# A third probability buffer, two rounds of lead and a fused masked maximum in the second block's attention

## Chip, cores and metric

The kernel is one program on one core of a Trainium2 chip, in fp32 throughout. The metric is the device time of one execution in microseconds, as the median of three runs.

## The reference, cut to what matters

The reference runs a first block (pooled mixing with chunk attention, a Mamba2 mixer, two mixture-of-experts layers) and then a second block of two layers. The change touches only the windowed attention of the second block's layers, and in layer 0 the attention of the 256 context positions, which the kernel treats as two more query tiles.

```python
def windowed_gqa(q, k, v, k_ctx, v_ctx, sink):        # 8 query heads, 2 key heads, head width 64
    # 4 query blocks of 128; keys: the block before, this one, the one after
    s_loc = jnp.einsum('bnqhgd,bnkhd->bnhgqk', qb, kw) * scale            # scale = 64 ** -0.5 = 0.125
    s_loc = jnp.where(mask, s_loc, NEG_INF)                # |key - query| <= 128, inside the sequence
    s_ctx = jnp.einsum('bnqhgd,bchd->bnhgqc', qb, k_ctx) * scale          # 256 context keys
    p = jax.nn.softmax(jnp.concatenate([s_loc, s_ctx, s_sink], axis=-1), axis=-1)
    o = einsum(p_loc, vw) + einsum(p_ctx, v_ctx)           # the sink has a share of p and no value
def context_attention(q, k, v, sink):                  # layer 0 only: 256 queries, 256 context keys
    p = jax.nn.softmax(jnp.concatenate([q k * scale, s_sink], axis=-1), axis=-1)[..., :L]
```

The same layers hold a depthwise convolution of 31 taps, gates (`att_z` among them, a product of the layer's input with a weight), retention, a short convolution and a merged output.

## The kernel before

Every engine runs its own program, written out by hand in program order; engines wait for each other by counting semaphores. A helper (`job`) hands out the eight PSUM banks of 512 columns in rotation: a new job waits until the bank's previous holder has been read.

The attention runs in rounds (n, j): a tile n of 128 queries and a key head j, which serves four query heads. Layer 0 has 12 rounds (4 sequence tiles, 2 context tiles, times 2 key heads), layer 1 has 8. Tiles 1 and 2 see three local key tiles, tiles 0 and 3 two, context tiles none; all see two context key tiles. PE's program per round (from L1310 on): scores of the next round (`att_scores`, L1294: a local part `sl`, L1304, and a context part `sx`, L1308, each a bank for each of the four heads), one part of the gate product `att_z` (L1290), then for each head the transposes of its normalised probabilities (L1330, two banks for each head), then the product with V (L1338, 64 output columns, into partitions 0 to 63 of one bank for each round).

DVE's program per round: `att_norm` (add the sink's exponential to the sums, L2128, reciprocal, L2930, scale each head's probabilities, L2124), `att_max` of the next round (for each head scale and add the mask, L2131, scale the context part, L2124; then one reduction over all four heads, L2134, the maximum with the sink, and two small results), three or four taps of the convolution of channel group 3 (`conv`, L2131), and now and then a gate product (L2131). ACT's program per round (L1980 on): the gate product's tanh and copy (`z_part_out`), copies of the transposes from PSUM to SBUF (L1575, two for each head), the four exponentials of the next round with their sums (L1567, each followed by a read of the accumulator), and two copies of the round's V product (L1575). All work in place in `pr2[r % 2]`, a buffer of 4 x 640 columns.

After the last round DVE makes the weight sums (`w_sums`, `w_sum_4`) and activation sums T1 to T4 of the next stage, whose first products (L716) PE starts at once.

Of the kernel before, what the change touches and what calls it, by code (L numbers as in the profile page):

```python
# [188 lines left out]
def program(nc, a, out, upto, old, new):  # L189

    ctx = ExitStack()
    with ctx:
# [18 lines left out]
        square = sb("square", [P, 2, S + L])  # L211
        rstd = sb("rstd", [P, S + L])
        part_sum = sb("part_sum", [P, 2, 3 * P])
# [257 lines left out]
        kd = mQ.take(2, S + L)  # L471
        k_raw = mQ.take(S + L)
        v_tok = mQ.take(6, P)
        cu = mQ.take(2, 813)
        pT2 = mQ.take(5, S)
        v_raw = arena[:, mQ.at - 5 * S:mQ.at - 5 * S + S + L]
        pr2 = [mQ.take(4, 640), None]
# [122 lines left out]
        def x_tiles(l):  # L600
            return range(6 if l == 0 else 4)

        def tile_at(n):

            return P * n
# [44 lines left out]
        def _(eng):  # L650
# [580 lines left out]
            if stage_on(6):  # L1231
                eng.wait_ge(small_landed, pe.at("small"))
                for l in range(2 if upto > 6 else 1):
# [59 lines left out]
                    def att_scores(n, j, z=()):  # L1293
                        for hh in range(4):  # L1294
                            if hh == 1:
                                for c, tag in z:
                                    z_bank[c, tag] = z_job(c, tag)
                            h = 4 * j + hh
                            po, c = 64 * (h % 2), h // 2
                            ql = q_[po:po + 64, c, n * P:(n + 1) * P]  # L1300
                            kt = key_tiles(n)
                            if kt:
                                b, full = job("sl", l, h, n)
                                nc.tensor.matmul(b[:, 0:P * len(kt)], ql,  # L1304
                                                        kd[po:po + 64, j, P * kt[0]:P * (kt[-1] + 1)],
                                                        start=True, stop=True).then_inc(tensor_done, pe.step(full))
                            b, full = job("sx", l, h, n)
                            nc.tensor.matmul(b[:, 0:L], ql, kd[po:po + 64, j, S:S + L], start=True, stop=True).then_inc(tensor_done, pe.step(full))  # L1308

                    z_bank = {}  # L1310
                    att_scores(*rounds[0])
                    for c, tag in z_parts(l, 0):
                        z_product(c, tag, *z_job(c, tag))
                    for r, (n, j) in enumerate(rounds):
                        if r + 1 < len(rounds):
                            att_scores(*rounds[r + 1], z=z_parts(l, r) if r else ())
                            for c, tag in z_parts(l, r) if r else ():
                                z_product(c, tag, *z_bank[c, tag])
                        kt = key_tiles(n)
                        nl = len(kt)  # L1320
                        for hh in range(4):
                            h = 4 * j + hh
                            eng.wait_ge(vector_done, pe.at(("pr2", l, n, h)))
                            pr = pr2[r % 2][:, hh, :]
                            for tag, t0, t1 in (("l", 0, nl), ("x", nl, nl + 2)):
                                if t1 == t0:
                                    continue
                                b, full = job("pt2", l, h, n, tag)
                                for t in range(t0, t1):
                                    mm = nc.tensor.transpose(b[:, (t - t0) * P:(t - t0 + 1) * P], pr[:, t * P:(t + 1) * P],  # L1330
                                                             C("ident"))
                                mm.then_inc(tensor_done, pe.step(full))
# [2041 lines left out]
```

## Time and profile before

| | us |
|---|---|
| median of 3 runs | 3477.21 (3474.63 to 3478.76) |
| span of the profiled execution, its own time in the profile | 3482.4 |
| PE busy | 3282.0 (94%) |
| DVE busy | 1790.9 (51%) |
| ACT busy | 901.8 (26%) |
| GpSimd busy | 287.3 (8%) |

PE is TensorE's matmul row, PEld its weight loads, DVE VectorE, ACT ScalarE. An fp32 matmul is two records in the trace, a transpose one. A record's time is longer than its slot, since matmuls are pipelined; the start of one to the start of the next is the slot. The profiled execution has no time beside its span; it lies 5.2 us above the median of the runs.

### The profile page before, as it was taken

The numbers are of one execution on the slowest core, as the hardware profiler recorded it, in microseconds if no ns is written. First come the engines' busy times: TensorE is split into PE (matmuls) and PEld (weight loads), VectorE is DVE, ScalarE is ACT, GpSimd is POOL, SyncE is SP. The second block draws the span as 40 slices with busy tenths as digits, with TensorE's granted clock in tenths as the row PEclk, the third lists the DMA queues.
The fourth block names the chain that finished last, engine by engine and source line by source line (L and its number), as shares of the span: only waits on it lengthen the run. The fifth ranks groups of instructions, "written<-read, shape, count | busy, mean of one in ns | idle before, by whom it ended". The sixth has DMA issues, their size and how long they took to land.

```text
span 3482.4 us, 36840 instructions
## 1 busy us (share of the span) xinstructions
PE 3282.0 (94%) x13516; PEld 2085.1 (60%) x13516; DVE 1790.9 (51%) x3363; ACT 901.8 (26%) x1855; POOL 287.3 (8%) x246
## 2 busy tenths in 40 slices
PE   8988989999998989989999999999999899999998
PEld 4743544778744545555555555555544556778887
DVE  2343226777713337777334454444468854554554
ACT  2241212344312221054231131111112523222222
POOL 1200421333101320000000000000000000000000
PEclk9988999999998999999999999999999999999999
DMA  8746876533355972101111212112221021222331
GB/s 271 227 138 204 341 272 214 176 86 97 115 174 202 363 269 61 37 13 41 37 49 39 58 43 66 56 55 61 61 64 58 19 65 45 65 72 80 85 91 61
DMA packets 418494, 394.00 MB, mean 113 GB/s; under 512 B 27888, under 2 KB 353648, under 8 KB 410896
## 3 DMA queue, kind: packets, MB, share of 16 engines
q1 hardware_dynamic: 384768, 348.01, 31.6%
q10 hardware_dynamic: 15120, 23.68, 2.1%
q0 software_dynamic: 18432, 19.98, 1.7%
q8 instruction: 111, 1.82, 0.2%
q14 instruction: 63, 0.52, 0.0%
HBM read 440.78 MB, written 31.52 MB: 136 GB/s over the span
## 4 chain that ended last, share of the span: by engine, by line
PE 61%; DVE 5%; ACT 3%; DMA 2%; issue 1%; ACTq 0%; DVEq 0%; POOL 0%; POOLq 0%
PE psum L716 38%; PE psum L701 6%; PE psum L1204 3%; PE psum L914 2%; DVE arena L2131 2%; PE psum L1290 2%; PE psum L1338 2%; ACT arena L1575 2%; DMA ring<-in_w_branch 1%; PE psum L933 1%; PE psum L1358 1%; PE psum L1370 1%; DVE arena L2128 1%; ACT arena L1567 1%; PE psum L899 1%
## 5 line engine op out<-in xcount | busy, mean ns | idle before, releaser
L716 PE MATMUL psum<-arena,ring 128*128 128x384 f32 (+1 forms) x2592 | 747.2, 439 | 12.8 <-DVE arena L2128 5.3
L716 PEld LDWEIGHTS psum<-arena,ring 128*128 128x128 f32 x2592 | 492.3, 191 | 238.6 <-DVE psum L2128 11.4
L716 PE MATMUL psum<-hT,ring 128*128 128x384 f32 (+1 forms) x2176 | 624.9, 440 | 2.3 <-ACT part_sum L1575 2.2
L716 PEld LDWEIGHTS psum<-hT,ring 128*128 128x128 f32 x2176 | 414.8, 191 | 192.7 <-issue 7.8
L1575 ACT ACTIVATE part_sum<-psum 128x256 f32<-128x256 f32 (+1 forms) x408 | 174.2, 429 | 953.4 <-PE psum L716 808.5
L2128 DVE TENSOR_TENSOR ring<-ring 128x512 f32<-128x512 f32 (+1 forms) x336 | 215.9, 662 | 260.1 <-PE psum L716 257.4
L2128 DVE TENSOR_TENSOR psum<-psum,part_sum 128x256 f32<-128x256 f32 (+1 forms) x328 | 156.2, 479 | 371.5 <-PE psum L716 262.7
L1575 ACT ACTIVATE arena<-psum 128x256 f32<-128x256 f32 (+5 forms) x501 | 210.5, 465 | 506.7 <-PE psum L701 188.8
L701 PE MATMUL psum<-hT,ring 128*128 128x512 f32 (+1 forms) x832 | 314.7, 540 | 14.1 <-DVE hT L2124 11.8
L1567 ACT ACTIVATE arena<-psum,cols 128x256 f32<-128x256 f32 (+3 forms) x280 | 131.7, 493 | 636.0 <-PE psum L914 195.3
L701 PEld LDWEIGHTS psum<-hT,ring 128*128 128x128 f32 x832 | 160.9, 194 | 167.8 <-issue 149.2
L2131 DVE SCALAR_TENSOR_TENSOR arena<-arena,vec 128x783 f32<-128x783 f32 (+1 forms) x256 | 228.7, 894 | 9.1
L2128 DVE TENSOR_TENSOR arena<-arena 128x512 f32<-128x512 f32 (+13 forms) x252 | 187.4, 757 | 58.1 <-DMA arena<-y_dram 18.4
L2131 DVE SCALAR_TENSOR_TENSOR arena<-arena,psum 128x384 f32<-128x384 f32 (+3 forms) x236 | 98.5, 447 | 217.2 <-ACT arena L1567 183.0
L1567 ACT ACTIVATE arena<-arena,cols 128x512 f32<-128x512 f32 (+8 forms) x199 | 158.6, 830 | 59.5 <-DVE arena L2131 24.5
L989 PE MATMUL psum<-hT,ring 128*128 128x256 f32 x672 | 154.4, 381 | 0.0
L989 PEld LDWEIGHTS psum<-hT,ring 128*128 128x128 f32 x672 | 126.4, 190 | 19.8 <-issue 3.4
L2128 DVE TENSOR_TENSOR arena<-psum,part_sum 128x384 f32<-128x384 f32 (+1 forms) x80 | 40.8, 510 | 164.1 <-PE psum L716 163.8
L716 PE MATMUL psum<-arena,square 128*128 128x384 f32 (+1 forms) x384 | 115.4, 436 | 3.8 <-DVE arena L2128 3.8
L1204 PE MATMUL psum<-arena,ring 128*128 128x512 f32 x256 | 111.8, 595 | 0.0
L914 PE MATMUL psum<-arena 128*64 128x256 f32 x960 | 108.8, 380 | 1.0 <-issue 1.0
L2131 DVE SCALAR_TENSOR_TENSOR xT<-psum,cols,xT 128x512 f32<-128x512 f32 (+1 forms) x64 | 37.7, 612 | 137.4 <-PE psum L1204 73.3
(255 smaller groups left out, 3693.3 us busy)
## 6 DMA issues: line engine op xcount, KB each, us to landing
ring<-in_w_in SPq DMA_DIRECT2D x172, 512.0 KB, 4.1
arena<-in_moe_w SPq DMA_DIRECT2D x44, 1536.0 KB
ring<-in_ada_w SPq DMA_DIRECT2D x96, 512.0 KB, 6.1
ring<-in_w_mod SPq DMA_DIRECT2D x48, 512.0 KB, 5.8
ring<-in_ssm_w_in SPq DMA_DIRECT2D x48, 512.0 KB, 5.5
ring<-in_w_branch SPq DMA_DIRECT2D x64, 256.0 KB, 3.1
hT<-in_moe_w SPq DMA_DIRECT2D x10, 1536.0 KB
ring<-in_moe_w SPq DMA_DIRECT2D x10, 1024.0 KB
```

What stands on the lines that cost most here:

```text
L701: mm = nc.tensor.matmul(b[:, 0:n], ws[k // 8][0][:, k % 8, :], rhs(k)[:, o:o + n], start=(k == 0), stop=(k == nk - 1))
L716: mm = nc.tensor.matmul(flat(bank_, nb), lhs[:, k, :], rhs(k), start=(start and k == 0), stop=(k == kd_ - 1), skip_group_check=True)
L899: mm = nc.tensor.transpose(b[:, j * P:(j + 1) * P], rows[:, i % DEEP, k * P:(k + 1) * P], C("ident"))
L914: mm = nc.tensor.matmul(b[LANES * h:LANES * h + LANES, 0:2 * P], rowsT[:, i % 2, k, LANES * h:LANES * h + LANES], step_weights(s, h, 2 * P ...
L989: mm = nc.tensor.matmul(bank_[:, 0:S // 2], lhs[:, k, :], rhs(k), start=(start and k == 0), stop=(k == 3), skip_group_check=True)
L1204: mm = nc.tensor.matmul(b, ws[k // 8][0][:, k % 8, :], yT[:, k, :], start=(k == 0), stop=(k == 15))
L1290: mm = nc.tensor.matmul(b[:, 0:w], z_w[c][0][:, k, :], hT[:, k, o:o + w], start=(k == 0), stop=(k == KD - 1))
L1338: mm = nc.tensor.matmul(b[0:64, :], v_tok[:, t, 64 * j:64 * j + 64], pT2[:, kb, :], start=(i == 0), stop=(i == len(tiles) - 1))
L1567: return nc.scalar.activation(out_, in_, f, bias=bias, scale=scale, **kw)
L1575: return nc.scalar.activation(out_, in_, ACT.Copy)
L2128: return v.tensor_tensor(out_, in0, in1, op)
L2131: return v.scalar_tensor_tensor(out_, in0, s, in1, op0, op1)
```

## The change

PE keeps two rounds of scores ahead instead of one; `pr2` gets a third buffer, over scratch that other stages use (`square`, `rstd`, part of `part_sum`, now one allocation). The context scores of four heads share two banks. Transposes go to one bank for each key tile, with the four heads side by side, so a bank is full only when the last head is done. ACT copies one bank of 512 columns for each key tile. The V product is made once for each tile, for both key heads, into the two halves of the partitions. On DVE one instruction scales, adds the mask, writes the scores and gives their running maximum, which starts from the sink (local part) or from the local part's maximum (context part, with a mask of zeros). The convolution taps and the gate product stand before `att_max`. ACT's `z_part_out` stands behind the exponentials. After the last round, T1 and T2 stand before the weight sums. The diff's core:

```diff
+        pT_window = arena[:, k_raw_at:k_raw_at + 3 * S].rearrange("p (a b) -> p a b", b=S)
+        pT_context = w_sum.rearrange("p m n -> p (m n)")[:, 0:2 * S].rearrange("p (a b) -> p a b", b=S)
+        pr2 = [mQ.take(4, 640), None, scratch[:, 0:4 * 640].rearrange("p (a b) -> p a b", b=640)]
...
+        def pr_no(l, r):
+            return (r + l) % 3
+        def pT2(j, kb):
+            return pT_first[:, kb, :] if j == 0 else pT_window[:, kb, :] if kb < 3 else pT_context[:, kb - 3, :]
...
+                    def att_turns(r, n, j):
+                        tiles = att_tiles(n)
+                        banks = [job("pt2", l, n, j, kb) for kb, t in tiles]
+                        for hh in range(4):
+                            eng.wait_ge(vector_done, pe.at(("pr2", l, n, 4 * j + hh)))
+                            for i, (b, full) in enumerate(banks):
+                                mm = nc.tensor.transpose(b[:, hh * P:(hh + 1) * P], pr2[pr_no(l, r)][:, hh, i * P:(i + 1) * P], C("ident"))
+                                if hh == 3:
+                                    mm.then_inc(tensor_done, pe.step(full))
+                    def att_values(n):
+                        tiles = att_tiles(n)
+                        b, full = job("av", l, n)
+                        for i, (kb, t) in enumerate(tiles):
+                            for j in range(2):
+                                eng.wait_ge(scalar_done, pe.at(("ptc2", l, n, j, kb)))
+                                mm = nc.tensor.matmul(b[64 * j:64 * j + 64, :], v_tok[:, t, 64 * j:64 * j + 64], pT2(j, kb),
+                                                      start=(i == 0), stop=(i == len(tiles) - 1), skip_group_check=True)
+                    att_scores(*rounds[1])
                     for r, (n, j) in enumerate(rounds):
+                        att_turns(r, n, j)
+                        if r + 2 < len(rounds):
+                            att_scores(*rounds[r + 2])
+                        for c, tag in z_parts(l, r) if r else ():
+                            z_product(c, tag, *z_job(c, tag))
+                        if j:
+                            att_values(n)
...
+                        for kb, t in att_tiles(n):
+                            jn = jobname("pt2", l, n, j, kb)
+                            eng.wait_ge(tensor_done, ac.at(("full",) + jn))
+                            copy(pT2(j, kb), bank(jn)).then_inc(scalar_done, ac.step([("free",) + jn, ("ptc2", l, n, j, kb)]))
                         if r + 1 < len(rounds):
                             att_exp(r + 1, *rounds[r + 1])
+                        if r:
+                            z_part_out(z_parts(l, r))
...
-                                stt(pr2[q][:, hh, 0:wl], b[:, 0:wl], 0.125, C("window", off, wl), ALU.mult, ALU.add).then_inc(vector_done, ve.step(free))
...
-                            ts(pr2[q][:, hh, wl:wl + L], b[:, 0:L], 0.125).then_inc(vector_done, ve.step(free))
...
-                        red(col("stat", 32 * q, 4), pr2[q][:, :, 0:wl + L], ALU.max).then_inc(vector_done, ve.step())
...
-                        tt(col("stat", 32 * q, 4), col("stat", 32 * q, 4), sink, ALU.max).then_inc(vector_done, ve.step())
+                            v.tensor_tensor_reduce(pr[:, hh, 0:wl], b[:, 0:wl], C("window", off, wl), 0.125, col("small", 16 + 8 * l + 4 * j + hh),
+                                                   ALU.add, ALU.max, top(hh)).then_inc(vector_done, ve.step([free, ("top", l, n, j, hh)]))
...
                         att_norm(r, n, j)
-                        if r + 1 < len(rounds):
-                            att_max(r + 1, *rounds[r + 1])
                         conv(3, taps * r, taps * r + taps)
...
+                        if r + 2 < len(rounds):
+                            att_max(r + 2, *rounds[r + 2])
```

## Rows read from the trace of the kernel before

**Rows 1.** The page's busy time of each engine over the span.
```profile
PE 3282.0 (94%) x13516; PEld 2085.1 (60%) x13516; DVE 1790.9 (51%) x3363; ACT 901.8 (26%) x1855; POOL 287.3 (8%) x246
```

**Rows 2.** Busy time by stretch: attention of layer 0, of layer 1.
```profile
core 0: us, PE busy (x) PEld busy (x) DVE busy (x) ACT busy (x) POOL busy (x), PEclk, DMA share, GB/s
1473.70:1625.50 151.80, 132.81 (x616) 85.23 (x616) 120.18 (x240) 76.34 (x234) 0.00 (x0) 0.98 0.05 15
2675.00:2791.30 116.30, 102.58 (x468) 64.85 (x465) 92.69 (x184) 57.43 (x166) 0.00 (x0) 0.96 0.06 19
```

**Rows 3.** Waits from 1503 to 1625 us: who for whom, total us, times, longest.
```profile
ACT arena L1567 <- PE psum L1290: 50.3, 10, 8.0
DVE cols L2128 <- ACT cols L1567: 21.1, 10, 3.6
PE psum L1338 <- ACT arena L1575: 12.1, 11, 1.3
PE psum L1330 <- ACT arena L1575: 3.3, 6, 0.6
```

**Rows 4.** Timeline of PE over a round: start, us, engine, line, operation, records.
```profile
1519.10 2.08 PE L1330 MATMUL psum<-const,arena 128*128 128x128 f32 x17 [0.51 <-ACT arena L1575]
1522.24 4.48 PE L1338 MATMUL psum<-arena 128*64 128x512 f32 x10 [1.07 <-ACT arena L1575]
1526.65 0.92 PE L1304 MATMUL psum<-arena 64*128 64x384 f32 x4
...
1529.11 3.72 PE L1290 MATMUL psum<-hT,ring 128*128 128x256 f32 x16
...
1533.67 0.55 PE L1330 MATMUL psum<-const,arena 128*128 128x128 f32 x3 [0.51 <-ACT arena L1575]
```

**Rows 5.** Timeline of PE: two-half products of an expert stage, one-half product of tile 3.
```profile
1170.79 1.94 PE L933 MATMUL psum<-arena 128*64 128x512 f32 x8
1172.56 3.62 PE L914 MATMUL psum<-ring,arena 128*64 128x256 f32 x32
...
1591.00 3.62 PE L1338 MATMUL psum<-arena 128*64 128x512 f32 x8 [1.25 <-ACT arena L1575]
```

**Rows 6.** Timeline of DVE over a round.
```profile
1511.04 0.16 DVE L2128 TENSOR_TENSOR cols<-cols 128x4 f32<-128x4 f32 x1 [3.63 <-ACT cols L1567]
...
1513.30 0.55 DVE L2131 SCALAR_TENSOR_TENSOR arena<-psum,const 128x384 f32<-128x384 f32 x1
1513.77 0.41 DVE L2124 TENSOR_SCALAR arena<-psum 128x256 f32<-128x256 f32 x1
...
1516.61 2.82 DVE L2134 TENSOR_REDUCE cols<-arena 128x4 f32<-128x2560 f32 x1
1519.46 0.16 DVE L2128 TENSOR_TENSOR cols<-cols 128x4 f32<-128x4 f32 x1
...
1519.92 3.17 DVE L2131 SCALAR_TENSOR_TENSOR arena<-arena,vec 128x783 f32<-128x783 f32 x3
1523.01 0.95 DVE L2131 SCALAR_TENSOR_TENSOR arena<-arena 128x768 f32<-128x768 f32 x1
```

**Rows 7.** Groups of DVE by line and form in a routing stage (mean ns last).
```profile
L2465 DVE TENSOR_TENSOR_SCAN arena<-arena,psum 32x512 f32<-32x512 f32 x1 | 1.2, 1207 | 0.7 <-PE psum L861 0.7
...
L2131 DVE SCALAR_TENSOR_TENSOR arena<-arena 32x512 f32<-32x512 f32 x1 | 0.7, 737 | 0.0
```

**Rows 8.** Timeline of ACT: a copy of 512 columns, one exponential, its read, the next.
```profile
1422.36 0.60 ACT L1575 ACTIVATE arena<-psum 128x512 f32<-128x512 f32 x1 [20.95 <-PE psum L701]
...
1521.82 0.87 ACT L1567 ACTIVATE arena<-arena,cols 128x640 f32<-128x640 f32 x1
1522.54 0.24 ACT L1567 ACTIVATION_READ_ACCUMULATOR arena<-arena,cols 128x1 f32 x1
1522.63 0.86 ACT L1567 ACTIVATE arena<-arena,cols 128x640 f32<-128x640 f32 x1
```

**Rows 9.** Timeline of PE: first transposes and next stage's first product, both layers.
```profile
1487.47 2.67 PE L1330 MATMUL psum<-const,arena 128*128 128x128 f32 x16 [0.89 <-DVE arena L2131]
...
1625.55 5.43 PE L716 MATMUL psum<-hT,ring 128*128 128x384 f32 x16
...
2688.77 2.66 PE L1330 MATMUL psum<-const,arena 128*128 128x128 f32 x16 [0.89 <-DVE arena L2131]
...
2791.31 3.72 PE L716 MATMUL psum<-hT,ring 128*128 128x256 f32 x16
```

More of the change, by code:

```diff
@@ new lines, in att_turns @@
+                    def att_turns(r, n, j):
[6 more added lines that the diff above has]
+                                if hh == 3:
+                                    mm.then_inc(tensor_done, pe.step(full))
@@ new lines, in att_values @@
+                    def att_values(n):
[6 more added lines that the diff above has]
+                                                      start=(i == 0), stop=(i == len(tiles) - 1), skip_group_check=True)
+                        mm.then_inc(tensor_done, pe.step(full))
@@ L1998, in _ @@
                         if r + 1 < len(rounds):
                             att_exp(r + 1, *rounds[r + 1])
-                        jn = jobname("av", l, n, j)
-                        eng.wait_ge(tensor_done, ac.at(("full",) + jn))
-                        bv = bank(jn)[0:64, :].rearrange("p (a b n) -> p a b n", a=2, b=2)
-                        for half in range(2):
-                            copy(br[64 * half:64 * half + 64, 12 + 2 * j:14 + 2 * j, tile_at(n):tile_at(n) + P],
-                                 bv[:, :, half, :]).then_inc(scalar_done, ac.step([("free",) + jn, ("att_o", l)]))
+                        if r:
+                            z_part_out(z_parts(l, r))
@@ new lines, in _ @@
+                        if j:
+                            jn = jobname("av", l, n)
+                            eng.wait_ge(tensor_done, ac.at(("full",) + jn))
+                            for jj in range(2):
+                                bv = bank(jn)[64 * jj:64 * jj + 64, :].rearrange("p (a b n) -> p a b n", a=2, b=2)
+                                for half in range(2):
+                                    copy(br[64 * half:64 * half + 64, 12 + 2 * jj:14 + 2 * jj, tile_at(n):tile_at(n) + P],
+                                         bv[:, :, half, :]).then_inc(scalar_done, ac.step([("free",) + jn, ("att_o", l)]))
@@ L2922, in att_max @@
-                        tt(col("stat", 32 * q + 12, 4), sink, col("stat", 32 * q, 4), ALU.subtract).then_inc(vector_done, ve.step(("nm2", l, n, j)))
+                        if r >= 3:
+                            eng.wait_ge(tensor_done, ve.at(("full",) + jobname("pt2", l, *rounds[r - 3], 4)))
+                        top = lambda hh: col("stat", 16 * q + hh)
+                        sink = col("small", 16 + 8 * l + 4 * j, 4)
+                        for hh in range(4 if kt else 0):
+                            off = P * (kt[0] - (n - 1))
+                            b, free = full("sl", l, 4 * j + hh, n)
+                            v.tensor_tensor_reduce(pr[:, hh, 0:wl], b[:, 0:wl], C("window", off, wl), 0.125, col("small", 16 + 8 * l + 4 * j + hh),
+                                                   ALU.add, ALU.max, top(hh)).then_inc(vector_done, ve.step([free, ("top", l, n, j, hh)]))
```

137 lines of the change are left out of this document (49 added, 88 removed).

## The prediction

> **What bounds the kernel now.** I read the page first: TensorE (PE) is busy for 94% of the span, VectorE (DVE) 51%, ScalarE (ACT) 26% [rows 1]. Those are averages. The change touches only the second block's attention, twice: 151.8 us in its layer 0 and 116.3 us in its layer 1. The table by stretches shows DVE at 120.2 and 92.7 us busy there, so two engines are loaded and not one [rows 2]. The waits of layer 0 give the pattern of a round (one tile of 128 queries, one key head): ACT waits for a gate product on PE, DVE waits for the exponentials, PE waits for the copies that ACT makes of the transposes [rows 3]. PE's own order shows the price: a full round repeats every 14.57 us (1519.10 to 1533.67), of which PE loses 0.51 and 1.07 us; the rest is transposes, 4.48 us for the product with V, 2.46 us of scores (1526.65 to 1529.11) and 3.7 us of gate product [rows 4]. So a shorter DVE or a longer lead alone can return about 1.6 us of a round; more must come from less PE work.
>
> **Less PE work: the product with V.** Its matmuls have 64 output columns. Now both key heads write partitions 0 to 63, one round after the other, and ten records of 512 columns take 4.48 us, 0.448 each [rows 4]. After, the two heads write the two halves of one bank, in turns, every second round. The trace has that form elsewhere: eight records of 512 columns into alternating halves take 1.94 us against 3.62 us for eight of one half, and 32 of 256 take 3.62 us, 0.113 each, where 16 full-width ones of 256 take 3.72 us [rows 5]. So pairs run side by side. There are 160 such records, 88 in layer 0 and 72 in layer 1; side by side they take 80 slots instead of 160, and 80 x 0.448 = 35.8 us of PE work goes. Transposes (0.115 us each, 17 in 2.08 less the 0.16 by which a record outlasts its slot), scores and gate products keep their number; the scores already run two heads side by side.
>
> **DVE per full round.** Now: scaling and masking 3.3 us (1513.30 to 1516.61), the maximum over four heads 2.85, three small operations 0.46, three convolution taps 3.1, a gate product of 0.95 every third round, normalisation 2.3 [rows 6]. After: eight fused instructions over the same elements, first taken at the old pitches of 0.47 and 0.33 us (3.2 us together), the 2.85 us reduction and one small operation gone. The fused form's price is not in the trace. Below: no more than the instruction it replaces. Above: the scan, the one DVE operation here that carries a running value from element to element, takes 1.21 us for 512 elements where a plain two-input one takes 0.74, so the rate may halve: 0.40 us more per 384 and 0.27 per 256, 2.7 us a full round [rows 7]. For reading out the running maximum, the nearest row is ACT's read of its accumulator: 0.24 us long, but the next exponential starts 0.09 us after it began [rows 8]. I take full rate, because the plain reduction, which also carries a maximum, takes 2.82 us for 2560 elements, one every 1.1 ns [rows 6], and 0.1 us per read. The maximum then costs 3.2 + 0.8 + 0.45 = 4.5 us instead of 6.6.
>
> The Trainium skill speaks against such a fusion: VectorE: DVE Perf Modes (Rules for kernel authors) says not to fuse chained operations for speed, since the flush between operations stays, but to lower their number. Here the number of instructions falls by two (a reduction and a maximum) and, counting accumulator reads as instructions of their own as the same page does (Two Vector instructions with no wait between them), it rises by six. By the rows what goes is a second pass of 2560 elements, so I expect a gain in spite of the rule.
>
> **ACT.** Per full round it now makes eight copies of 384 and 256 columns; after, five of 512, at 0.60 us long each [rows 8], 0.52 from start to start by the 0.08 by which one copy overlaps the next. The exponentials are unchanged: 0.81 each and 0.32 for the sink, 3.55 us. But a bank now holds one key tile of all four heads, so the first copy starts only when the last head is transposed. That latency was partly hidden and is now exposed.
>
> **Following the new order.** E is the moment at which the last head of a round is transposed.
> From an even round (no V product) to the next: ACT copies 2.7, exponentials 3.55, DVE normalisation 2.35, last head's transposes 0.7: 9.4 us. DVE's own work (3.1 + 4.5 + 2.35 = 10.0) fits because its taps are done ahead, while PE is late; only in the first pair of rounds does DVE set this step, again 9.4.
> From an odd round to the next, PE sets it: the scores two rounds ahead wait for banks that ACT's third copy frees (1.7), finish in 0.9, gate product 3.7, V products 10 slots = 4.5, next round's transposes 20 x 0.115 = 2.3: 13.1 us. A pair takes 22.5 us instead of 29.1.
> With two local key tiles (tiles 0 and 3) V takes 8 slots (3.6) and four transposes a head fewer, so the steps are 9.4, 12.2 for rounds 0 to 2, 9.4, 13.1, 9.4 for 2 to 5, 12.7 and 8.1 for 5 to 7: 74.3 us. Layer 0 has four context rounds more: 9.6, 5.9, 7.9, 5.3 by the same parts, then 3.0 for the last copies and V product: 31.7. Layer 1 ends with 4.2.
> At the start, normalisation of round 0 now stands behind the maximum of round 1, whose scores come after two gate products: the first normalisation ends some 1.5 us later.
> Before, from the last transpose of round 0 to the next stage's first product it is 135.4 us in layer 0 (1490.14 to 1625.55) and 99.9 us in layer 1 (2691.43 to 2791.31) [rows 9]. After: 74.3 + 31.7 + 1.5 = 107.5, and 74.4 + 4.2 + 1.5 = 80.1. Gains 27.9 and 19.8.
> The weight sums (2.6 us on DVE) now follow the last V product, while two of the activation sums come before it; PE has two products of its own (5.3 us in layer 0, 3.7 in layer 1) to cover them. In layer 1 I charge 1.0 us. In sum 46.7 us.
> The third buffer costs nothing by itself: it lies over scratch idle in this stage. No DMA is added. Later stages move up whole.
> The profiled execution has its span of 3482.4 us; 3482.4 - 46.7 = 3435.7. The runs' median is 3477.2, 5.2 less, so the forecast is 3430.5, said as 3431.
>
> **Rivals.**
> 1. The fused instruction runs at half rate. A full pair is then set by DVE: 2 x (3.1 + 0.3 + 7.2 + 2.35) = 25.9 us, 3.4 worse, four times; the eight rounds with two local tiles lose some 2 us a pair and the context rounds 3 in all: 14 + 8 + 3 = 25 us of the gain, time 3456. For it: the scan. Against: the reduction's pace. The Trainium skill has a rule of this kind in Vector Engine (DVE) Microarchitecture Reference (Points that are easy to get wrong): instructions of this class with two SBUF sources that are not bf16 run at half throughput; here one source is PSUM, and no row shows the case.
> 2. The V products don't pair, because each waits for copies of either head, or because PSUM is shared: the 35.8 us come back and 11 stay, time 3466. The pairs of rows 5 speak against it; the copies are 4 us old when the products start.
> 3. DVE gets slower than before: each fused instruction over 1.0 us. The place is the running maximum's path, and the point is clear: a full round has 14.57 - 10.3 = 4.3 us to give, 0.53 us on each of eight. At three times the reduction's pace (some 1.45 us for 384 and 1.05 for 256, read included) the round takes 16.3 us, 1.7 more, and with two tiles 14.4 against some 12: 14 + 16 = 30 us worse, less the 5 that ending PE's waits gives: 3502. Nothing in the trace is that slow.
> 4. The change gives more: ACT's copies overlap better and the bank wait is short. PE's busy time in both stretches is 235.4 us [rows 2]; less 35.8 it is 199.6 of 268.1, so at most 68 us can go: 3409.
> 5. The lead is not used: the scores two rounds ahead get their banks late, so DVE's taps never run ahead and the copies hold PE. Then an even round takes 3.1 + 4.5 + 2.35 + 0.7 = 10.7 instead of 9.4 and an odd one waits 1.0 more; ten pairs of rounds times 2.3 are 23 us, time 3454. For it: eight banks against thirteen bank uses in a round with V products.
>
> **From these to numbers.** My account 0.55, half rate 0.13, no pairing 0.07, lead lost 0.10, more gain 0.10, slower 0.03, no change through several of these at once 0.02. The range takes in rivals 1, 4 and 5 at their prices: 3410 to 3460. The likeliest case alone has 3422 to 3442. A change under 0.2%, 7 us, can't be told from none; faster 0.95, same 0.02, slower 0.03.
>
> **What would show it.** V products: ten records in about 2.3 us. The fused rows at 0.55 and 0.42 us with a short accumulator read behind; near 0.95 and 0.7 means rival 1. PE's waits: none for copies before V, but 2 to 3 us before transposes in even rounds, released by DVE. Pair of full rounds at 22.5 us. First product of the next stage 26 us (layer 0) and 46 us (both) earlier in the span. If the fused form is above 1 us, or a pair takes 27 us or more, I am wrong.

## The result and the profile after

The kernel after takes 3428.8 us (median of four runs, 3423.2 to 3435.3), the kernel before 3476.1: a ratio of 0.9868 with a 95% interval of 0.9851 to 0.9885. The forecast was 3431. Five more runs of the same kernel on another chip gave 0.9858 (0.9841 to 0.9876), so the gain is 46 to 49 us. The profiled execution, the slowest of the four, has a span of 3433.3 us where 3435.7 was worked out. Its page shows 43 us less PE busy time [rows 1]:

```profile
PE 3239.1 (94%) x13516; PEld 2069.9 (60%) x13516; DVE 1753.1 (51%) x3467; ACT 895.2 (26%) x1791; POOL 287.3 (8%) x246
```

Nearly the whole gain lies in the two attention stages. By stretches, each from its first scores to the next stage's first product (layer 0, layer 1; columns as in [rows 2]):

```profile
1476.66:1597.01 120.35, 109.25 (x616) 76.06 (x616) 98.36 (x294) 73.17 (x196) 0.00 (x0) 0.99 0.06 18
2643.09:2744.12 101.03, 90.29 (x472) 63.67 (x472) 75.93 (x230) 54.31 (x136) 0.00 (x0) 0.89 0.07 21
```

They were 151.8 and 117.6 us ([rows 2] begin layer 1 at 2675.00, 1.3 us behind its first scores at 2673.67), so 31.5 and 16.6 us went, 48.1 of the 49.1 by which the span fell. Over these same stretches PE's busy time was 132.9 and 103.9 us; it fell by 23.6 and 13.6 us, 37.2 in sum. The rest, 10.9 us, is idle time of PE. Of the page's 43 us of busy time, 5.7 lie outside the two stages, where the span changed by 1.0: sums of busy time can differ here by some microseconds without as much gain in time. The next stage's first product comes 28.5 us earlier in the span in layer 0 and 47.2 in layer 1, where 26 and 46 were expected.

PE's timeline over two full rounds: transposes, scores (local, context), gate product; then the same with the V product of both heads.

```profile
1511.74 2.41 PE L1331 MATMUL psum<-const,scratch 128*128 128x128 f32 x20
1514.08 1.56 PE L1315 MATMUL psum<-arena 64*128 64x384 f32 x8
1515.53 1.14 PE L1320 MATMUL psum<-arena 64*128 64x256 f32 x8
1516.59 3.72 PE L1306 MATMUL psum<-hT,ring 128*128 128x256 f32 x16
1520.91 2.38 PE L1331 MATMUL psum<-const,arena 128*128 128x128 f32 x20 [0.59 <-ACT arena L1583]
...
1525.73 3.72 PE L1306 MATMUL psum<-hT,ring 128*128 128x256 f32 x16
1529.38 3.23 PE L1341 MATMUL psum<-arena 128*64 128x512 f32 x13
...
1533.82 2.40 PE L1331 MATMUL psum<-const,arena 128*128 128x128 f32 x20
```

The pair takes 22.08 us (1511.74 to 1533.82) with a single wait of 0.59; before it took twice 14.57 [rows 4]. Twenty V records take 4.44 us (1529.38 to 1533.82) instead of 2 x 4.48. DVE's timeline of the fused maximum, each with its accumulator read, and the small operations up to the normalisation:

```profile
1515.14 0.62 DVE L2924 CUSTOM_DVE_ANT_0 arena<-psum,const,cols 128x384 f32<-128x384 f32 x1 [0.23 <-PE psum L1315]
1515.68 0.08 DVE L2924 DVE_READ_ACCUMULATOR2_ANT cols<- 128x1 f32 x1
1515.68 0.61 DVE L2924 CUSTOM_DVE_ANT_0 arena<-psum,const,cols 128x384 f32<-128x384 f32 x1
...
1517.30 0.48 DVE L2931 CUSTOM_DVE_ANT_1 arena<-psum,const,cols 128x256 f32<-128x256 f32 x1
1517.70 0.08 DVE L2931 DVE_READ_ACCUMULATOR2_ANT cols<- 128x1 f32 x1
1517.70 0.48 DVE L2931 CUSTOM_DVE_ANT_1 arena<-psum,const,cols 128x256 f32<-128x256 f32 x1
...
1519.03 0.17 DVE L2136 TENSOR_SCALAR cols<-cols 128x4 f32<-128x4 f32 x1
...
1519.79 0.16 DVE L2140 TENSOR_TENSOR cols<-cols 128x4 f32<-128x4 f32 x1 [0.53 <-ACT cols L1583]
...
1520.20 1.94 DVE L2136 TENSOR_SCALAR arena<-arena,cols 128x640 f32<-128x640 f32 x4
```

From one fused instruction to the next it is 0.54 us for 384 elements and 0.40 for 256, read included; the old plain ones had 0.47 and 0.33. The maximum with its small operations takes 4.1 us (1515.14 to 1519.27) instead of 6.6 [rows 6]. Behind it DVE stands idle for 0.53 us, until ACT's exponentials are done, and then normalises. So in this even round the maximum is not the last thing that is waited for, but it has only half a microsecond to spare.

The profile puts PE's wait of 0.59 us down to ACT's L1583. The row of that line which ends there (from 1520.35, 0.47 long) is the gate product's tanh, and the transposes have no need of it: they take the five banks that follow the gate product's, and otherwise wait for DVE's normalisation of the first head. It began at 1520.20, 0.71 us before them; at the start of layer 0, where the profile does name DVE, that distance is 0.64 us, for heads of 512 columns and not 640. The wait is DVE's.

At the start of each layer there is now a loss. PE's first two transposes (layer 0, then layer 1) and the next stages' first products:

```profile
1490.97 2.62 PE L1331 MATMUL psum<-const,arena 128*128 128x128 f32 x16 [3.28 <-DVE arena L2136]
1500.28 1.94 PE L1331 MATMUL psum<-const,arena 128*128 128x128 f32 x16 [3.38 <-DVE arena L2136]
...
1597.01 5.43 PE L732 MATMUL psum<-hT,ring 128*128 128x384 f32 x16
...
2660.35 3.65 PE L1331 MATMUL psum<-const,arena 128*128 128x128 f32 x16 [3.28 <-DVE arena L2136]
2670.69 3.65 PE L1331 MATMUL psum<-const,scratch 128*128 128x128 f32 x16 [3.20 <-DVE scratch L2136]
...
2744.12 3.72 PE L732 MATMUL psum<-hT,ring 128*128 128x256 f32 x16
```

PE waits over 3 us before each, where the first wait was 0.89 [rows 9]. In layer 1 sixteen transposes then take 3.65 us, both times at a granted clock of 0.50, where the same number takes 1.94 at 1.00. The granted clock of the two first stretches of 20.9 us of layer 1 was, after:

```profile
2643.10:2664.00 20.90, 17.62 (x82) 14.38 (x82) 11.59 (x46) 4.91 (x15) 0.00 (x0) 0.74 0.09 25
2664.00:2684.90 20.90, 17.70 (x80) 11.32 (x80) 18.49 (x58) 10.71 (x28) 0.00 (x0) 0.78 0.00 1
```

and before it was 0.88 and 0.92:

```profile
2675.00:2695.90 20.90, 19.32 (x86) 13.03 (x85) 14.97 (x34) 9.09 (x28) 0.00 (x0) 0.88 0.09 26
2695.90:2716.80 20.90, 18.17 (x76) 11.40 (x75) 17.14 (x36) 8.85 (x27) 0.00 (x0) 0.92 0.00 1
```

So more of the stretch runs at the lower of the clock's two levels (1.2 GHz and not 2.4), behind waits of 3.3 us. Such a wait doesn't bring the low level each time: in layer 0 of the same execution the transposes behind waits of 3.28 and 3.38 us had 0.71 and 1.00, and took 2.62 and 1.94 us.

### The profile page after: what moved, and what is told of

Read it like the earlier page. It is cut to its first block, busy times and chain, and to the rows that moved or that the text cites. A ratio compares the mean times of both kernels' runs of the same rounds, so it can differ in the third digit from the quotient of the medians.

```text
span 3433.3 us, 36838 instructions
## 1 busy us (share of the span) xinstructions
PE 3239.1 (94%) x13516; PEld 2069.9 (60%) x13516; DVE 1753.1 (51%) x3467; ACT 895.2 (26%) x1791; POOL 287.3 (8%) x246
## 4 chain that ended last, share of the span: by engine, by line
PE 62%; DVE 5%; DMA 2%; ACT 2%; issue 1%; POOL 0%; DVEq 0%; ACTq 0%; POOLq 0%
PE psum L732 38%; PE psum L717 6%; PE psum L1220 3%; PE psum L930 2%; DVE arena L2143 2%; PE psum L1306 2%; DMA ring<-in_w_branch 1%; PE psum L949 1%; PE psum L1374 1%; PE psum L1386 1%; PE psum L1331 1%; PE psum L1341 1%; DVE arena L2140 1%; ACT arena L1591 1%; PE psum L915 1%
## 5 line engine op out<-in xcount | busy, mean ns | idle before, releaser
L1591 ACT ACTIVATE scratch<-psum 128x256 f32<-128x256 f32 (+1 forms) x408 | 173.9, 429 | 951.2 <-PE psum L732 806.8
L2140 DVE TENSOR_TENSOR psum<-psum,scratch 128x256 f32<-128x256 f32 (+1 forms) x328 | 155.9, 480 | 370.7 <-PE psum L732 263.1
L1591 ACT ACTIVATE arena<-psum 128x512 f32<-128x512 f32 (+5 forms) x417 | 195.4, 499 | 540.8 <-PE psum L717 189.1
L1583 ACT ACTIVATE arena<-psum,cols 128x256 f32<-128x256 f32 (+3 forms) x280 | 131.5, 492 | 565.1 <-PE psum L930 230.4
L1583 ACT ACTIVATE arena<-arena,cols 128x512 f32<-128x512 f32 (+10 forms) x171 | 138.8, 841 | 54.3 <-DVE arena L2143 22.9
L2140 DVE TENSOR_TENSOR arena<-psum,scratch 128x384 f32<-128x384 f32 (+1 forms) x80 | 40.9, 511 | 162.1 <-PE psum L732 162.1
L732 PE MATMUL psum<-arena,scratch 128*128 128x384 f32 (+1 forms) x384 | 113.9, 432 | 3.8 <-DVE arena L2140 3.8
```

The costliest lines, as they stand in the source:

```text
L732: mm = nc.tensor.matmul(flat(bank_, nb), lhs[:, k, :], rhs(k), start=(start and k == 0), stop=(k == kd_ - 1), skip_group_check=True)
L1583: return nc.scalar.activation(out_, in_, f, bias=bias, scale=scale, **kw)
L1591: return nc.scalar.activation(out_, in_, ACT.Copy)
L2140: return v.tensor_tensor(out_, in0, in1, op)
```

## The experiments

**Theory:** PE's own work sets the full rounds after the change, DVE has time to spare, and the V product's shorter time is most of the gain. **Rival:** DVE's shorter maximum, or the lead, is what brings it, and PE had slack. All times are medians; gain is (1 - ratio) x 3475 us, each ratio against runs of the kernel before on the same chip. "Stages" is the two stretches from first scores to next stage's first product, from the profile.

| kernel | us | ratio (95%) | gain | stages |
|---|---|---|---|---|
| after | 3428.8 | 0.9868 (0.9851 to 0.9885) | 46 | 120.4 + 101.0 |
| after, run again | 3425.0 | 0.9858 (0.9841 to 0.9876) | 49 | 120.4 + 101.0 |
| 1 V heads in turn, same bank | 3438.9 | 0.9891 (0.9874 to 0.9908) | 38 | 134.6 + 103.0 |
| 2 maximum not fused | 3445.3 | 0.9913 (0.9893 to 0.9933) | 30 | 134.4 + 106.0 |
| 3 lead of one | 3439.0 | 0.9891 (0.9860 to 0.9922) | 38 | 132.4 + 103.4 |
| 4 before, V paired | 3481.0 | 1.0020 (1.0008 to 1.0032) | -7 | 152.4 + 123.8 |
| 5 before, maximum fused | 3462.8 | 0.9972 (0.9959 to 0.9985) | 10 | 147.3 + 114.7 |
| 6 V heads in banks apart | 3456.1 | 0.9943 (0.9924 to 0.9962) | 20 | 142.9 + 111.3 |
| 7 lead alone | 3477.1 | 1.0009 (0.9997 to 1.0021) | -3 | 149.6 + 122.5 |
| 8 no convolution taps | 3428.3 | 0.9869 (0.9844 to 0.9893) | 46 | 127.1 + 96.1 |
| 9 first softmaxes earlier | 3424.5 | 0.9862 (0.9844 to 0.9880) | 48 | 121.0 + 97.9 |
| 10 and one gate product moved | 3421.2 | 0.9848 (0.9833 to 0.9863) | 53 | 120.0 + 94.9 |
| 11 and a second one | 3411.7 | 0.9819 (0.9806 to 0.9833) | 63 | 116.7 + 91.3 |

**1. The V product's heads one after the other.**

```diff
-                        for i, (kb, t) in enumerate(tiles):
-                            for j in range(2):
+                        for j in range(2):
+                            for i, (kb, t) in enumerate(tiles):
```

> The changed kernel, but the V product of a tile runs all key tiles of key head 0 and then all of key head 1, so that no two neighbouring records write different halves. My theory (less TensorE work is the main gain): a full tile's V product takes 20 slots of 0.43 us, 9 us instead of 4.4, and because TensorE sets the step after an odd round, nearly all of the 35 us come back: about 3464 us. Rival (the lead and the fused maximum are the gain, TensorE has room): less than 15 us come back, under 3444 us.

Neither number came. PE's timeline of the twenty V records in this kernel:

```profile
1532.19 5.43 PE L1341 MATMUL psum<-arena 128*64 128x512 f32 x16
1537.45 1.88 PE L1341 MATMUL psum<-ring,arena 128*64 128x512 f32 x4
1539.27 1.97 PE L1331 MATMUL psum<-const,arena 128*128 128x128 f32 x16
```

They take 7.1 us, not 9.0: some four records of the one half still run beside the other's, though the order no longer alternates. The full pair takes 24.71 instead of 22.08, that is 2.63 more, just what the V product takes more (7.08 less 4.44). The ablation was partial; PE sets the odd step all the same. Run 6 makes it whole. The stages don't show the same split: layer 0 grew by 14.2 us and layer 1 by 2.0, since in this profile the first transposes ran at the low clock in layer 0 (3.65 us twice) and less so in layer 1 (2.82 and 1.94).

**2. The maximum not fused**, with the other parts kept.

```diff
-                            v.tensor_tensor_reduce(pr[:, hh, 0:wl], b[:, 0:wl], C("window", off, wl), 0.125, ..., ALU.add, ALU.max, top(hh))
+                            stt(pr[:, hh, 0:wl], b[:, 0:wl], 0.125, C("window", off, wl), ALU.mult, ALU.add)
...
+                        red(col("stat", 16 * q, 4), pr[:, :, 0:wl + L], ALU.max)
+                        tt(col("stat", 16 * q, 4), col("stat", 16 * q, 4), sink, ALU.max)
```

> The changed kernel, but the scores are scaled and masked by one instruction, and the maximum is taken by a reduction over the four heads and a maximum with the sink, as in the kernel before; third buffer, lead and paired V product stay. My theory: VectorE gets 2.5 us more in a full round (12.4 instead of 9.9 us), so a pair of full rounds is set by VectorE at about 24.8 us instead of 22.1; with the rounds of fewer key tiles and the start this costs some 27 us: about 3456 us. Rival (the lead of two rounds hides VectorE's work): under 8 us, under 3437 us.

3445 us is less loss than the theory's 3456 and more than the rival's 3437. The waits before transposes grew, in the start and in the full rounds (PE's timeline):

```profile
1483.75 3.65 PE L1331 MATMUL psum<-const,arena 128*128 128x128 f32 x16 [5.22 <-DVE arena L2136]
...
1521.58 4.50 PE L1331 MATMUL psum<-const,arena 128*128 128x128 f32 x20 [3.31 <-DVE arena L2136]
```

The wait for DVE in the step from an even round to the next grew from 0.59 to 3.31 us, and behind it the twenty transposes take 4.50 us instead of 2.38, at a granted clock of 0.50, and the next scores 0.6 us more: nearly as much again as the wait itself. In the second pair of full rounds the wait is 1.58 us, and the transposes behind it are not slower.

In the first of these two steps DVE's own load counts too: it has no gap from 1501.12 to 1526.03 us. Its maximum starts at 1513.97, as soon as the taps and the gate product ahead of it are done, 1.94 us behind the start of the scores; in the kernel after it starts 1.06 us behind that, and waits for them. In the second pair it waits 0.50 us for the scores.

**3. A lead of one round** (PE's scores and DVE's maximum of round r + 1 in round r; third buffer and banks kept).

```diff
-                        att_turns(r, n, j)
-                        if r + 2 < len(rounds):
-                            att_scores(*rounds[r + 2])
+                        if r + 1 < len(rounds):
+                            att_scores(*rounds[r + 1])
...
+                        att_turns(r, n, j)
```

> The changed kernel with one round of lead instead of two, in the order of the kernel before (scores of the next round and gate product ahead of the transposes; maximum of the next round right behind the normalisation, gate evacuation ahead of the copies). My theory: the transposes' banks are then those of the next round's scores, so the transposes wait for VectorE's maximum and a round is one chain of 13.2 us: maximum of the local part 2.2, transposes 2.4, copies 2.7, exponentials 3.55, normalisation 2.35; a full pair takes 26.4 us, about 30 us are lost in all: 3459 us. Rival (the lead brings nothing of its own): within 5 us of the changed kernel, about 3430 us.

In between: waits for DVE of 4.24 and 3.70 us in the steps from an even to an odd full round, and 8 to 11 us lost in all by the ratios. DVE's and ACT's order went back to that of the kernel before along with PE's, so this is the price of the lead with its order.

**4. The kernel before with only the V product paired.**

```diff
-                        b, full = job("av", l, n, j)
+                        if j:
...
+                            b, full = job("av", l, n)
...
+                            for i, (kb, t) in enumerate(tiles):
+                                for jj in range(2):
```

> The kernel before with the V product alone changed: once for a tile, for both key heads into the two halves, in turns; a second tile of transposed probabilities takes the place of idle memory, and the weight sums at the end stand behind the last V product. One round of lead, two buffers and the separate reduction stay. My theory: TensorE's work falls by 35 us, but VectorE's 12.5 us a round then set the pace (25.5 to 26 us a full pair instead of 29.1): about 25 us gained, 3451 us. Rival (pairing alone brings all of it): 3440 us or less. Rival (nothing without the lead): over 3470 us.

PE's busy time is 35 us less (3247.3), and the kernel is slower. It took the side of the rival that expected next to nothing without the lead. PE's timeline, rounds without a V product:

```profile
1486.74 1.22 PE L1315 MATMUL psum<-arena 64*128 64x256 f32 x2 [5.74 <-DVE arena L2142]
...
1518.12 1.22 PE L1315 MATMUL psum<-arena 64*128 64x256 f32 x2 [4.76 <-DVE arena L2142]
...
1550.20 1.22 PE L1315 MATMUL psum<-arena 64*128 64x256 f32 x2 [5.05 <-DVE arena L2142]
```

PE stands ahead of the last head's context scores (L1315 here, two records), for a bank that holds the first head's local scores of the same round: in the kernel before, the scores of a round take eight banks, all there are, and from the second round on the gate product takes a ninth among them. DVE's maximum must have read that bank first, and in DVE's order it stands behind the normalisation, which waits for ACT's exponentials. With a V product in each round PE reached this point later; in the kernel before the same wait is 1.01 us at 1498.22, and there is none in the full rounds that [rows 4] show.

**5. The kernel before with only the fused maximum** (the new instruction in place of the masked copy, the context copy and the reduction, in the old order; one small maximum joins the two parts of each head).

> The kernel before with the fused instruction alone (masked copy and running maximum of each head's local and context part; one small maximum joins the two parts); order, lead, two buffers and unpaired V product stay. My theory: TensorE sets a round at 14.6 us and its waits there are for ScalarE's copies, so VectorE's 2.5 us a round are hidden: at most 6 us gained, over 3470 us. Rival (VectorE is the bound): 20 us or more, under 3456 us.

10 us: between the two. DVE's busy time fell by 37 us (1754.3), so most of the saving lies beside other work when nothing else changes.

**The same kernel again**, beside runs 5, 9 and 10 on one chip.

> The changed kernel once more, beside the next three on one chip: about 3429 us, ratio to the kernel before 0.987.

**6. V products in banks apart**, both in partitions 0 to 63.

```diff
-                        b, full = job("av", l, n)
-                                mm = nc.tensor.matmul(b[64 * j:64 * j + 64, :], v_tok[:, t, 64 * j:64 * j + 64], pT2(j, kb),
+                        for j in range(2):
+                            b, full = job("av", l, n, j)
+                                mm = nc.tensor.matmul(b[0:64, :], v_tok[:, t, 64 * j:64 * j + 64], pT2(j, kb),
```

> The kernel after, but the V product of each key head goes into a bank of its own, both into partitions 0 to 63, so that no two of its records can run beside each other (in the earlier ablation, which changed only the order, the trace showed 20 records in 7.1 us, that is some four records still alongside). Theory (PE sets the rounds; its own work is the largest gain): the full tile's V product takes 20 x 0.45 = 9.0 us instead of 4.4, tiles 0 and 3 16 x 0.45 = 7.2 instead of 3.5, a context tile 3.6 instead of 1.8; 4 x 4.5 + 4 x 3.6 + 2 x 1.8 = 35.8 us more over both layers, with no wait to hide it: 3425 + 36 = 3461 us. Rival (DVE sets the rounds, and PE had slack that takes it): under 3445.

Nearer the theory's 3461 than the rival's 3445: 26 to 31 us worse than the kernel after. Twenty records now take 8.73 us (1527.00 to 1535.73):

```profile
1527.00 7.09 PE L1341 MATMUL psum<-arena 128*64 128x512 f32 x16
1533.92 1.88 PE L1341 MATMUL psum<-ring,arena 128*64 128x512 f32 x4
1535.73 1.53 PE L1331 MATMUL psum<-const,arena 128*128 128x128 f32 x12
```

**7. Lead alone**: edits 2 and 6 together.

> The kernel after with both of the other parts taken out: V products apart (as in the run before last) and the unfused masked copy, context copy, one reduction and maximum with the sink. What is left of the change is the third buffer, the two rounds of lead, the transposes by key tile and the copies of 512. If the parts only added (fusing 20 us, pairing 36 us, both measured by taking them out alone), it takes 3425 + 20 + 36 = 3481 us, slower than before: the lead would be worth nothing. Theory (a round takes the longer of PE and DVE, and with V products apart PE is by far the longer): the unfused maximum is hidden in the full rounds, only the start shows it, 5 to 8 us: 3461 + 7 = 3468 us, so the lead alone gains some 7 us against before.

My theory fell here: the unfused maximum was not hidden by PE's longer work; against run 6 it cost 21 to 23 us, no less than with paired products (16 to 19). PE's timeline over a full pair of it:

```profile
1513.09 2.41 PE L1331 MATMUL psum<-const,scratch 128*128 128x128 f32 x20
...
1524.07 3.88 PE L1331 MATMUL psum<-const,arena 128*128 128x128 f32 x20 [2.40 <-DVE arena L2136]
...
1534.04 7.09 PE L1341 MATMUL psum<-arena 128*64 128x512 f32 x16
```

The V product now stands in odd rounds alone, so an even round is short on PE, whatever V costs: scores, maximum and normalisation must fit in it, and the slack of the odd one doesn't help. DVE waits 2.42 us for the scores before this maximum, and PE 2.40 us for the normalisation behind it. The pair takes 29.7 us (1513.09 to 1542.77), no less than the 29.1 of before: the 3.2 us of waits that the lead took from it came back as a wait for DVE and slow transposes.

**8. Without the convolution taps 1 to 29 of channel group 3** (left out of the rounds).

```diff
-                        conv(3, taps * r, taps * r + taps)
+                        if r == 0:
+                            conv(3, 0, 1)
+                        if r == len(rounds) - 1:
+                            conv(3, 30, 32)
```

> The kernel after, with the convolution taps 1 to 29 of channel group 3 left out of DVE's rounds (so that output is not the reference's). It takes 3 to 4 products of 32x512, 2.2 to 2.9 us, from DVE in each round. Theory (PE sets the full rounds, DVE has a spare): pairs of full rounds stay at 22.1 us; only the waits at the start of each layer (3.3 + 3.4 us, taps of round 0 stand ahead of the second maximum) and in context rounds shrink, some 8 to 10 us in all: 3416 us. Rival (DVE is still the bound of the rounds): 12 x 2.9 + 8 x 2.2 = some 50 us, of which at least half shows: 3400 or less.

No gain, neither the theory's 3416 nor the rival's 3400: 50 us less DVE work (1702.8 busy) are worth nothing. The full pair stays at 22.1 us (1507.10 to 1529.17), so DVE's load is no bound there. The stages shift by a few us between the layers, since in this profile the granted clock fell in layer 0 (0.74 and 0.78) and less in layer 1; the sum moved by 1.8 us. Nor do the taps cause the start's waits, which stay at 3.29 and 3.24 us in layer 0: DVE waits for PE, before the second maximum and again before the third (DVE's timeline):

```profile
1487.79 0.62 DVE L2924 CUSTOM_DVE_ANT_0 scratch<-psum,const,cols 128x384 f32<-128x384 f32 x1 [3.55 <-PE psum L1315]
```

What holds at the start is a chain: scores, maximum, normalisation behind it in DVE's order, transposes, next scores. In the full rounds of the kernel after, DVE has its 0.53 us to spare with or without the taps. Together with run 2 this says that DVE's load is no bound with the fused maximum, and that a maximum 2.5 us longer is more than the rounds can hide. It doesn't say that only the chain counts in run 2: there the taps delay the maximum in one of the steps, and a kernel with the unfused maximum and without the taps was not run.

**9. The start in another order**: normalisation of round 0 ahead of the maximum of round 1, that of round 1 ahead of the maximum of round 2.

```diff
+                    att_norm(0, *rounds[0])
                     att_max(1, *rounds[1])
...
-                        att_norm(r, n, j)
+                        if r >= 2:
+                            att_norm(r, n, j)
...
+                        if r == 0:
+                            att_norm(1, *rounds[1])
                         if r + 2 < len(rounds):
                             att_max(r + 2, *rounds[r + 2])
```

> The changed kernel with VectorE's order altered at the start of each attention: normalisation of round 0 ahead of the maximum of round 1, and normalisation of round 1 ahead of the maximum of round 2. My theory: in the changed kernel TensorE waits 3.3 us before the transposes of rounds 0 and 1 each because these normalisations stand behind a maximum that nobody needs yet; the order saves about 3.5 us in layer 0 and, since TensorE's clock fell to 0.74 there, some more in layer 1: about 8 us, 3421 us. Rival (the exponentials end last anyway): within 3 us of the changed kernel.

The wait moved and did not go: 1.58 us before the first transposes, but 5.90 before the second (3.28 and 3.38 in the kernel after; layer 0). In time no difference can be told.

**10. One gate product from ahead of the rounds into round 0**, and the first exponentials ahead of its evacuation.

```diff
-            return each[0:2] if r == 0 else each[r + 1:r + 2]
+            return each[r + 1:r + 2]
```

> The same order, and in addition one of the two gate products at the start moved into round 0, where TensorE waits for the normalisation of round 1, and the first exponentials ahead of the first gate evacuation on ScalarE. My theory: transposes of round 1 start about 5.5 us earlier than in the changed kernel in layer 0 and more in layer 1: about 12 us, 3417 us. Rival: the start is limited by VectorE's own work, and moving the gate product gains nothing over the order alone.

The waits become 1.64 and 2.79 us in layer 0, 2.74 and 2.79 in layer 1. The gain is 4 us against the kernel after on the same chip, with intervals that overlap; 3417 was expected. The stages of the profile are 6.5 us shorter.

**11. One more gate product ahead of the rounds, taken from round 3**, an odd full round (against run 10).

```diff
-            return each[r + 1:r + 2]
+            return [] if r == 3 else each[r + 2:r + 3] if r < 3 else each[r + 1:r + 2]
...
-            return [(0, "x0")]
+            return [(0, "x0"), (0, "x1")]
```

> The run with the fuller start (3421 us, its gate product in round 0 and the first two softmaxes ahead of the next maximum), with one more gate product taken from round 3, an odd full round, and put ahead of the second round's scores at the start. The order of DVE and ACT stays. In round 3 PE's step falls by one gate product, 3.65 us, from 12.9 to 9.2, as long as an even one, so nothing should stall there. Theory (the start is set by the chain scores, maximum, exponential, normalising, and only more work of PE's own ahead of it fills it): the waits before the first turns (1.6 us in layer 0, 2.7 in layer 1) go, and those before the second (2.8 us in each) shrink by what PE comes later, 1 to 2 us: 3.5 us in each layer, 3414 us. Rival (the first turns wait for a bank that the second maximum frees, or round 3 now waits): within 2 us of 3421.

The best version, 3411.7 us. PE's timeline of layer 1's first two transposes and next stage:

```profile
2644.99 1.97 PE L1335 MATMUL psum<-const,arena 128*128 128x128 f32 x16
...
2655.76 3.48 PE L1335 MATMUL psum<-const,scratch 128*128 128x128 f32 x16 [2.80 <-DVE cols L2926]
...
2723.92 3.72 PE L736 MATMUL psum<-hT,ring 128*128 128x256 f32 x16
```

The wait before the first is gone (2.74 us in run 10; 1.64 in layer 0, gone too), the one before the second stayed at 2.80 and did not shrink; the stages lost 3.3 and 3.6 us against run 10, near the 3.5 expected, in layer 1 with 0.9 of it from the last sixteen transposes (1.94 instead of 2.87 us). Round 3 now takes 9.5 us in layer 0, with a wait of 0.18 behind it (10.1 and 0.72 in layer 1). Against the kernel after, layer 1's stage is 9.8 us shorter, more than the waits: the granted clock of its first two stretches of 20.9 us is 0.93 and 0.92, where it was 0.74 and 0.78.

```profile
2632.60:2653.50 20.90, 20.30 (x112) 16.25 (x112) 13.60 (x52) 10.04 (x28) 0.00 (x0) 0.93 0.09 25
2653.50:2674.40 20.90, 18.64 (x103) 12.90 (x104) 19.38 (x61) 11.49 (x28) 0.00 (x0) 0.92 0.09 26
```

## Why the prediction was right, step by step

**PE work.** 35.8 us were to go; PE's busy time in the two stages fell by 37.2, which also holds what the clock did, and taking the pairing out whole (run 6) cost 26 to 31 us of time and 33 of the two stages. Right.

**DVE's maximum.** 4.5 us forecast, 4.1 measured: the pitch rose by 0.07 for each read, where 0.1 was charged. Full rate was right, and half rate (rival 1, priced at 25 us) is excluded by the 0.54 us. That its length costs time is shown by runs 2 and 7 (16 to 23 us); that this is by the chain alone is not shown, since DVE's load takes part in run 2. So the rule of the Trainium skill that chained operations are not to be fused for speed (VectorE: DVE Perf Modes, Rules for kernel authors) does not hold here: the same fusion brought 10 us in the kernel before and 16 to 23 with the lead, since a pass over 2560 elements went.

**The rounds.** Pair of full rounds 22.5 forecast, 22.1 measured; even step 9.4 against 9.2 (the parts named for it, 2.7, 3.55, 2.35 and 0.7, add up to 9.3); odd step 13.1 against 12.9. In the odd step the 1.7 us of waiting for copies and 0.9 of finishing show as 2.5 us in which the scores run almost without a stop. From the last transpose of round 0 to that of round 7: 74.3 forecast, 72.1 in layer 0 and 75.7 in layer 1, where the second transposes ran at the low clock. Context rounds and tail 31.7, measured 31.3; layer 1's end 4.2 and 1.0 for the weight sums, measured 4.4 together.

**The start.** Charged at 1.5 us a layer. From first scores to the last transpose of round 0 it went from 16.4 to 16.9 in layer 0 (0.5), and from 17.76 to 20.91 in layer 1 (3.2). The split does not fit, since the clock was left out. In layer 1 the transposes ran at its low level. In layer 0 it hid a part of the cost: the first two gate products take 7.17 us after and took 8.13 before, with a granted clock of 1.00 and 0.88, so 1.0 us of the later start was given back. The start is the term that was most mis-sized in layer 1: 18.8 us gained by the forecast, 16.6 measured; layer 0 made it good with 31.5 against 27.9. That the two errors offset each other, so that the sum came within 1.4 us (46.7 against 48.1), is luck.

**PE's waits.** "2 to 3 us before transposes in even rounds, released by DVE" had the size wrong for the full rounds and the releaser right: 0.59 us, for a normalisation that itself stands behind ACT's exponentials. The step's own sum had said it: 9.4 us less 8.5 of PE work (2.3 of transposes, 2.5 of scores, 3.7 of gate product) leaves 0.9. Waits of the forecast size came at the start, 3.2 to 3.4 us, and before the last transposes of layer 1:

```profile
2736.95 2.73 PE L1331 MATMUL psum<-const,scratch 128*128 128x128 f32 x16 [2.43 <-DVE scratch L2136]
```

**Rivals.** No pairing was priced at 3466; measured 3456. Lead unused was 3454; a lead of one gives 3439. That the lead alone or a shorter DVE alone would be worth at most 1.6 us a round was right as a bound (run 7: nothing; run 5: 10 us over twenty rounds).

**What the forecast did not see is that the parts need each other.** Gains in us, from the table:

| | no lead | with the lead |
|---|---|---|
| neither | 0 | -3 |
| fused | 10 | 20 |
| paired | -7 | 30 |
| both | 38 | 46 to 49 |

(The "both, no lead" kernel has the new banks and third buffer; the others without lead have the old ones, so the left column mixes in the bank layout. By the program, sharing the context banks leaves the scores of a round at six banks instead of eight, so that they no longer meet their own first bank; no run has that change without the new transposes.) The sum of single gains is 0; together they make 46 to 49.

## What to carry to other kernels

Work taken from the busiest engine is a gain only where the buffers let it run on: look for the bank or buffer that is asked for next before counting it. An engine that is busy half of the time can still end a wait: before a step on it is made longer or shorter, look how long it stands idle between that step and the next thing it needs (here 0.53 us). Where PE waits for a chain at the start of a stage, move PE work there from rounds that have it to spare (run 11). And a wait on TensorE may cost more than itself: behind waits of 3.2 to 3.4 us the low clock added between nothing and 2.8 us to the transposes and scores that followed.

## What the hardware showed unexpectedly

Two products into different partition halves ran partly side by side although ten records of the one stand in the program before the first of the other: 7.1 us for twenty, against 4.4 in turns and 8.7 in the same half. With four records of each (a context tile) the order made no difference. The page TensorEngine Tiling (Array Packing) of the Trainium skill says under Key Properties that tiles work independently; how far ahead in the order they may lie it does not say, and these rows give about four records of 512 columns (7.08 us are sixteen slots of 0.44 for twenty records).

The fused masked maximum, with one source in PSUM, costs 0.54 and 0.40 us for 384 and 256 elements, 0.07 more than the plain instructions of the same size. Its accumulator read is 0.08 us long and starts together with the next fused instruction; that the read accounts for the 0.07 is likely and not shown.
